# A rebuilt prologue and conv stage in a one-core decoder-trunk step

## The reference

```python
h = x * rsqrt(mean(x * x) + EPS) * norm_mix            # per token
a = h @ w_pw1 + b_pw1                                  # 1024 -> 2048
glu = a[..., :1024] * sigmoid(a[..., 1024:])
full = concat([hist, glu], axis=1)                     # 30 rows of history: zeros (prompt), state (samples)
c = silu(layernorm(causal_dwconv(full, w_dw, b_dw)))   # width 31, one filter per channel
x = x + (c @ w_pw2 + b_pw2)
```

## Time and profile before

| | |
|---|---|
| median of 3 runs | 2673.03 us (2672.75 to 2674.61) |
| span of the profiled execution, first to last instruction | 2671.8 us |
| mean granted TensorE clock | 0.957 |
| TensorE matmul busy (PE) / weight load (PEld) | 2464.1 us (92%) / 2360.2 us (88%) |
| VectorE, ScalarE, GpSimd busy | 1352.7 / 528.5 / 772.3 us |
| PE on the chain that ended last | 82% of the span |

### The profile page before, as it was taken

One profiled execution on the slowest core, in us unless ns is written; L12 is line 12 of the kernel. 1 busy time (PEld: TensorE's weight loads), 2 busy tenths in 40 slices (PEclk: granted clock), 3 DMA queues, 4 the chain that ended last, 5 costly groups with the idle time before them and its releaser, 6 DMA issues.

```text
span 2671.8 us, 37036 instructions
## 1 busy us (share of the span) xinstructions
PE 2464.1 (92%) x14763; PEld 2360.2 (88%) x14763; DVE 1352.7 (51%) x1227; ACT 528.5 (20%) x914; POOL 772.3 (29%) x400
## 2 busy tenths in 40 slices
PE   3899995699999999999989989889999999999996
PEld 2888884699999999999979967679999999999996
DVE  2688887534444444344464656644444433444444
ACT  2432221421011110111030057612111011011113
POOL 0132321332333333333322223322333333333320
PEclk9898987799999999999999979988999999999998
DMA  5010100111111111111111020011111111111111
GB/s 162 24 32 16 31 16 8 40 40 40 48 47 47 40 47 47 47 47 47 40 39 40 16 60 1 9 32 40 40 48 47 47 41 45 47 47 47 41 38 70
DMA packets 156781, 110.93 MB, mean 42 GB/s; under 512 B 6487, under 2 KB 142055, under 8 KB 156599
## 3 DMA queue, kind: packets, MB, share of 16 engines
q1 hardware_dynamic: 154352, 98.90, 14.4%
q10 hardware_dynamic: 2371, 11.21, 1.4%
HBM read 105.20 MB, written 8.10 MB: 42 GB/s over the span
## 4 chain that ended last, share of the span: by engine, by line
PE 82%; DVE 9%; ACT 3%; issue 3%; DMA 1%; ACTq 1%; DVEq 0%; POOL 0%
PE PS L1398 53%; PE PS L1416 15%; PE PS L1501 5%; DVE CONV L778 2%; PE PS L1289 2%; PE PS L1450 2%; PE PS L1320 2%; PE PS L1292 1%; DVE X L693 1%; ACT WK L1147 1%; DVE WK L874 1%; DMA WK<-in_state_ffn 1%; PE PS L1557 1%; PE PS L1523 1%; DVE WK L666 1%
## 5 line engine op out<-in xcount | busy, mean ns | idle before, releaser
L1398 PE MATMUL PS<-H,W 128*128 128x344 f32 x9504 | 1531.3, 323 | 47.6 <-DVE H L854 21.9
L1398 PEld LDWEIGHTS PS<-H,W 128*128 128x128 f32 x9504 | 1518.0, 190 | 54.4 <-issue 34.2
L450 POOL CAST W<-RAW 128x1024 fp32r<-128x1024 f32 x176 | 195.2, 1109 | 1580.1 <-issue 782.1
L1416 PE MATMUL PS<-MID,W 128*128 128x344 f32 x3168 | 513.7, 322 | 20.4 <-DVE X L693 10.5
L1416 PEld LDWEIGHTS PS<-MID,W 128*128 128x128 f32 x3168 | 504.5, 190 | 27.0 <-DVE X L693 16.5
L452 POOL TENSOR_TENSOR W<-RAW,W 128x1024 fp32r<-128x1024 f32 x176 | 477.8, 2715 | 14.1
L693 DVE TENSOR_TENSOR X<-PS,X 128x1032 f32<-128x1032 f32 (+1 forms) x184 | 226.2, 1230 | 231.2 <-PE PS L1416 183.4
L778 DVE SCALAR_TENSOR_TENSOR CONV<-WK,PAR,CONV 128x1024 f32 (+1 forms) x152 | 223.9, 1473 | 18.0 <-DVE CONV L778 2.0
L898 DVE TENSOR_TENSOR WK<-PS,WK 128x1032 f32<-128x1032 f32 x44 | 54.3, 1233 | 299.9 <-PE PS L1398 297.6
L1154 ACT ACTIVATE MID<-WK 128x1032 fp32r<-128x1032 f32 x44 | 47.1, 1070 | 678.2 <-DVE WK L900 678.2
L874 DVE TENSOR_TENSOR WK<-PS,WK 128x1032 f32<-128x1032 f32 x44 | 54.3, 1233 | 224.0 <-PE PS L1398 223.9
(11 more groups left out here) (173 smaller groups left out, 1547.8 us busy)
## 6 DMA issues: line engine op xcount, KB each, us to landing
RAW<-in_ffn_w_in SPq DMA_DIRECT2D x176, 256.0 KB, 3.9
RAW<-in_ffn_w_down SPq DMA_DIRECT2D x88, 256.0 KB, 3.8
RAW<-in_conv_w_pw SPq DMA_DIRECT2D x48, 256.0 KB, 4.0
RAW<-in_attn_w_qkv SPq DMA_DIRECT2D x24, 256.0 KB, 3.8
XIN<-in_x_prompt ACTq DMA_DIRECT2D x8, 512.0 KB, 13.2
RAW<-in_attn_w_o SPq DMA_DIRECT2D x32, 128.0 KB, 2.8
out_y_prompt<-YOUT SPq DMA_DIRECT2D x8, 512.0 KB
WK<-in_const_rope ACTq DMA_DIRECT2D x1, 1032.0 KB, 5.3
```

The costliest lines, as they stand in the source:

```text
L450: nc.gpsimd.tensor_copy(W[:, slot, 0, :], RAW[:, slot, :]).then_inc(s_hi, hi.up())
L1398: last = matmul(PS[:, 3 * side + c, 0:CH], W[:, slot, wp, k * P:(k + 1) * P], H[:, hp, k, c * CH:(c + 1) * CH], start=(k == 0 and q == 0), ...
L1416: last = matmul(PS[:, 3 * side + c, 0:CH], W[:, slot, wp, t * BANK + m * P:t * BANK + (m + 1) * P], MID[:, t, hp, c * CH:(c + 1) * CH], st ...
```

## The change

- **Loads.** SP issues x blocks 0 to 3, the first pw1 weight tile, x blocks 4 to 7, the second weight tile, then history rows, a repeated copy of the depthwise weights (`WREP`) and the FFN rows. Each x block has its own semaphore. ScalarE issues 12 row DMAs instead of 20; the four state copies move behind the making of `H`.
- **x, block by block.** TensorE transposes a token block as it lands. ACT squares the same block with a running sum along the row, so token sums need no matmul; `RS` is ready before the first dense group.
- **Normalised H.** DVE makes `X * norm_mix * RS` (`normed_tile`), ACT its high part, DVE its rest. Dense results need no scaling: ACT's sigmoid and DVE's gated product read PSUM directly.
- **First two dense groups together** (`dense_pair`): for each tile of `H`, as it comes, the matmuls of both sides.
- **Late parameters.** FFN rows are transposed after that pair; the sample history becomes a product on POOL and 16 small matmuls (`SHIST`).
- **Taps one tile behind.** TensorE runs both dense groups of tile i, then `last_taps(i - 1)`. DVE does the gated product, 8 taps (NEARLY), `finish_tile(i - 1)`, the rest of `GSPLIT`, 11 taps. The loops are written out straight. Single buffers stay single.

```diff
+            for b in range(NB // 2):
+                x_block(b)
             load(halves(w_pw1, 0), 0)
+            for b in range(NB // 2, NB):
+                x_block(b)
             load(halves(w_pw1, D), 1)
...
+            pool.wait_ge(s_hrows, 16 * HROW_DMAS)
+            for hf in range(2):
+                nc.gpsimd.tensor_tensor(HROWS[hf], HROWS[hf], WREP[0:HALF_B * HIST, :], ALU.mult).then_inc(s_hw, 1)
...
+            for b in range(NB):
+                o = b % 2
+                dve.wait_ge(s_tr, tr.next())
+                v.tensor_copy(X[:, :, b * P:(b + 1) * P].rearrange("p (a m) n -> p a m n", a=2),
+                              PS[:, 2 * o:2 * o + 2, :].rearrange("p a (m n) -> p a m n", m=KT // 2)).then_inc(s_trr, trr.up())
...
+            token_scale()
+            dve.wait_ge(s_bc, bc.next())
+            v.tensor_copy(RS[:, 0:SEQ].rearrange("p (c n) -> p c n", c=2), PS[:, 6:8, :])
+            v.tensor_copy(RS[:, SEQ:T], PS[:, 5, 128:128 + NS]).then_inc(s_bcr, bcr.up())
...
+            def normed_tile(m):
+                v.scalar_tensor_tensor(NORMED[m % 2], X[:, m, :], par(m, R_MIX), RS, ALU.mult, ALU.mult).then_inc(s_n32, n32.up())
+            def normed_lo(m):
+                dve.wait_ge(s_hh, hh.next())
+                v.tensor_tensor(H[:, 1, m, :], NORMED[m % 2], H[:, 0, m, :].bitcast(F32), ALU.subtract).then_inc(s_h, h.up())
+            normed_tile(0)
+            normed_tile(1)
+            for m in range(KT):
+                normed_lo(m)
+                if m + 2 < KT:
+                    dve.wait_ge(s_h, h.at())
+                    normed_tile(m + 2)
...
+            def gated_tile(i):
+                mm.n += 2
+                dve.wait_ge(s_sig, sig.next())
+                if i > 0:
+                    dve.wait_ge(s_gh, gh.at())
                 dve.wait_ge(s_v, own.at())
+                v.scalar_tensor_tensor(chunks(GL[:, HIST:WKC]), side(0), par(i, R_B1), chunks(SIG), ALU.add,
+                                       ALU.mult).then_inc(s_pr, pr.up(2))
...
+            for i in range(KT):
+                gated_tile(i)
+                if i == 0:
+                    late_params()
+                v.scalar_tensor_tensor(CONV[:, i, SEQ:T], GL[:, HIST + SEQ:WKC], par(i, R_DW + HIST), SHIST[:, i, :],
+                                       ALU.mult, ALU.add).then_inc(s_v, own.up())
+                dve.wait_ge(s_tap0, tap0.next())
+                conv_taps(i, 1, 1 + NEARLY)
+                if i > 0:
+                    finish_tile(i - 1)
                 dve.wait_ge(s_gh, gh.next())
                 v.tensor_tensor(GSPLIT[:, 1, 0:WKC], GL[:, 0:WKC], GSPLIT[:, 0, 0:WKC].bitcast(F32), ALU.subtract).then_inc(s_gs, gs.up())
+                conv_taps(i, 1 + NEARLY, CW - NT)
             finish_tile(KT - 1)
...
+            act.wait_ge(s_rows, 16 * ROW_DMAS)
+            F_(JUNK[1][0:NS, :], XS_ROWS, ACT.Square, accum_out=TOK[0:NS, 0, NB:NB + 1]).then_inc(s_a, 1)
+            for b in range(NB):
+                act.wait_ge(s_xb[b], 16)
+                if b > 0:
+                    act.wait_ge(s_a, b)
+                F_(JUNK[b % 2], XIN[:, b, :], ACT.Square, accum_out=TOK[:, 0, b:b + 1]).then_inc(s_a, 1)
...
+            for i in range(KT):
+                act.wait_ge(s_mm, 2 * i + 2)
...
+                F_(chunks(SIG), PS[:, 3:6, 0:CH], ACT.Sigmoid, bias=par(i, R_B1 + 1)).then_inc(s_sig, sig.up())
                 act.wait_ge(s_pr, pr.next(2))
+                F_(CONV[:, i, 0:SEQ], GL[:, 0:SEQ], ACT.Identity, scale=par(i, R_DW), bias=par(i, R_BDW)).then_inc(s_tap0, tap0.up())
+                F_(CKEEP[:, i, :], GL[:, SEQ:WKC], ACT.Copy)
+                if i == 0:
+                    act.wait_ge(s_late, 1)
+                else:
+                    act.wait_ge(s_td, td.next())
                 F_(GSPLIT[:, 0, 0:WKC], GL[:, 0:WKC], ACT.Copy).then_inc(s_gh, gh.up())
+                diagonals(i, DIAGA, 0)
                 diagonals(i, DIAGB, NTA)
...
+            for b in range(NB):
+                o = b % 2
+                pe.wait_ge(s_xb[b], 16)
+                if b >= 2:
+                    pe.wait_ge(s_trr, trr.next())
+                for m in range(KT):
+                    last = transpose(PS[:, 2 * o + m // 4, (m % 4) * P:(m % 4 + 1) * P], XIN[:, b, m * P:(m + 1) * P])
                 last.then_inc(s_tr, tr.up())
...
+            def dense_pair():
+                for n in range(2):
+                    pe.wait_ge(s_w, w.next())
+                    begin_group()
+                for k in range(KT):
+                    pe.wait_ge(s_h, h.next())
+                    for side in range(2):
...
+            def late_params():
+                pe.wait_ge(s_frows, 16 * FROW_DMAS)
+                for f in range(FT):
+                    transpose(PS[:, 7 - f // 12, (f % 12) * 2 * NFR:(f % 12 + 1) * 2 * NFR], FROWS[0:2 * NFR, f * P:(f + 1) * P])
+                pe.wait_ge(s_hw, 2)
+                for m in range(KT):
+                    for hf in range(2):
+                        col = 400 + m * NS + hf * HALF_B
+                        last = matmul(PS[:, 6, col:col + HALF_B], HROWS[hf][:, m * P:(m + 1) * P], KSEL, start=True, stop=True)
+                last.then_inc(s_late, 1)
...
+            dense_pair()
+            late_params()
+            for i in range(1, KT):
+                pe.wait_ge(s_pr, 2 * i)
+                dense(0, 0, wait_taken=False)
+                dense(1, 1, wait_taken=False)
+                last_taps(i - 1)
+            last_taps(KT - 1)
```

More of the change, by code:

```diff
@@ L232, in build @@
         s_rows = sem("rows_loaded")
-        s_x = sem("x_loaded")
+        s_xb = [sem(f"x_block_loaded{b}") for b in range(NB)]
+        s_frows = sem("ffn_rows_loaded")
+        s_hrows = sem("history_rows_loaded")
+        s_hw = sem("history_weighted")
+        s_late = sem("late_params_turned")
+        s_latr = sem("late_params_taken")
+        s_n32 = sem("normed_tile")
         s_tab = sem("tables_loaded")
@@ L441, in _, with split @@
             raw = [Count(), Count()]
-            def split(slot, per, free):
+            def split(slot, per, free, first_pair=False):
                 pool.wait_ge(s_raw[slot], raw[slot].next(per))
-                if free:
+                if free and not first_pair:
                     pool.wait_ge(s_wstart, started.at())
@@ L749, in _ @@
[L749 to L761, removed]
@@ new lines, in normed_lo @@
+            def normed_lo(m):
[8 more added lines that the diff above has]
+                    normed_tile(m + 2)
+            sig, glu, tap0, gh, gs, td, tt = (Count() for _ in range(7))
@@ L1024, in _ @@
[L1024 to L1028 removed]
+                    (XS_ROWS, a["x_sample"].rearrange("b s d -> (b s) d")),
@@ L1084, in diagonals @@
                     F_(D_[:, 0, k, :], IDENT, ACT.Identity, scale=par(i, R_DW + CW - NT + first + k))
-                    lo = TAPLO[:, bass.ds(i, 1), first + k:first + k + 1].rearrange("p a b -> p (a b)")
-                    last = F_(D_[:, 1, k, :], IDENT, ACT.Identity, scale=lo)
+                    last = F_(D_[:, 1, k, :], IDENT, ACT.Identity, scale=TAPLO[:, i, first + k:first + k + 1])
                 last.then_inc(s_diag, diag.up())
-            GL, TG, SIG = (WK[:, k, :] for k in (4, 3, 5))
@@ L1235, in _ @@
                     roots()
-            turned, taken = 1 + KT, 2 + KT
+            turned, taken = TURNED, TAKEN
             ka = Count()
@@ L1464, in _ @@
-            for m in range(KT):
-                last = transpose(PS[:, 7, m * NS:(m + 1) * NS], WK[0:NS, 3, m * P:(m + 1) * P])
-            last = matmul(PS[:, 7, 64:64 + NH], ONES[0:1, :], WK[0:1, 3, D:D + NH], start=True, stop=True)
-            last.then_inc(s_tr, tr.up())
-            pe.wait_ge(s_trr, trr.next(2))
-            pe.wait_ge(s_x, 16 * NB)
-            for m in range(KT):
-                o = m % 2
-                pe.wait_ge(s_trr, trr.at(1))
-                trr.n += 1
-                for b in range(NB):
-                    last = transpose(PS[:, 2 * o + b // 4, (b % 4) * P:(b % 4 + 1) * P], XIN[:, b, m * P:(m + 1) * P])
-                last.then_inc(s_tr, tr.up())
@@ L1503, in last_taps @@
                 last.then_inc(s_td, td.up())
-            dense(0, 0)
-            last_taps()
-            dense(1, 1)
-            with turns(pe, 2, KT, {w: 2, started: 2, mm: 2, pr: 2, gs: 1, diag: 2, td: 1, tt: 1}):
-                dense(0, 0)
-                last_taps()
-                dense(1, 1)
-            last_taps()
+            dense_pair()
+            late_params()
+            for i in range(1, KT):
+                pe.wait_ge(s_pr, 2 * i)
[3 more added lines that the diff above has]
+            last_taps(KT - 1)
             pe.wait_ge(s_cs, KT)
```

284 lines of the change are left out of this document (129 added, 155 removed).

## The result

The changed kernel takes 2601.43 us (median of four runs, 2599.74 to 2603.38); the kernel before takes 2672.89 on the same chip (2669.36 to 2674.61). The ratio is 0.9734, 95% interval 0.972 to 0.9748: 71.5 us faster, against 74 to 75 predicted. The profiled execution took 2603.38 us, its span is 2601.6, its mean granted clock 0.967.

The account below looks back on a forecast made before the run. Matmuls fill 92% of the span, so gains come only where TensorE waits, does needless work or runs below full clock, in the first 450 us. Prologue 40.2 plus tiles 41.7 less tail 7.9 gives 74 us off: 2598, range 2580 to 2626.

Parts of the forecast that it names:

- the first transpose at 20 us or later: Prologue: a sign that the prediction is wrong; the rows were forecast to be in at 12 us.
- rows in: Prologue: the 12 parameter rows land at 12 us, between a lower bound of 8 and an upper one of 28.1.
- small operations, transposes of x: Prologue: 17 small operations take 3.2 us, 64 transposes of x 15.9, ending at 31.1; PE sets this.
- to the first dense matmul: Prologue: last copy, reciprocal, broadcasts, copies to `RS`, two `normed_tile`, one rest and hand-overs; the dense pair starts at 41.
- dense pair: Tile 0's first two dense groups: 22.7 us plus 2.6 for PE's slow start, ending at 66.3 against 106.46.
- late parameters and pair 1: Between tile 0 and tile 1: 9.0 us of transposes and small matmuls on PE, then pair 1 in 22.7.
- six tiles: After pair 1: six times taps and pair at 38.25 us, 229.5 in all; the eighth pair ends at 327.5.
- tail: Eighth pair's end to first layer-norm sum: 49 us, near the 51 with DVE late; 43 with DVE on time.
- rows come late: Prologue rival: rows still land at 28.1 because x competes; everything up to the pair moves by 16, 2614; chance 0.12.
- The estimate from that page: 31-row load on one engine: 4.4 us alone, 8.8 with x in between; rows in near 14, sum 2 us higher.
- a stream swinging between the two levels: Dense pair rival: small pauses keep the clock low; the pair takes 36.5 instead of 25.3, 2609 us; chance 0.07.
- straight code that comes too slowly: Tiles 2 to 7 rival: PE instructions delivered too slowly; above 10.6 us a tile the time passes 2673; chance 0.03.

Follow-up runs that it names:

- both remedies together: Against the changed kernel, the 31-row load is cut into 16 and 15 rows and x waits for the parameter rows: 2592.37 us, ratio 0.9710.

## Why the prediction was right

The total was right by 3.4 us, and the mark at the layer-norm sum by 0.2 (376.5 forecast, 376.68 measured). In part this is chance: terms too large and too small cancelled, and one of the forecast's own signs of being wrong came true (the first transpose at 20 us or later; it stands at 22.42).

| Step | forecast | measured | off by |
|---|---|---|---|
| rows in | 12 | 22.42 | +10.4 |
| small operations, transposes of x | 19.1 | 14.4 | -4.7 |
| to the first dense matmul | 9.9 | 12.1 | +2.2 |
| dense pair | 25.3 | 24.35 | -1.0 |
| late parameters and pair 1 | 31.7 | 32.7 | +1.0 |
| six tiles | 229.5 | 228.8 | -0.7 |
| tail | 49 | 41.9 | -7.1 |

**Rows at 12** was the step that failed most. I put them near the lower bound because the bulky rows had left the queue; what mattered was one 31-row load with x beside it. With x held back the rows are in at 11.2, so two thirds of the rival "rows come late" came true (10.4 of its 16 us). Its sum, 2614, did not come, because other terms fell. By the rule that the prediction cites from the Trainium skill ("DMA: Bandwidth & Descriptors", "Why a DMA increments its semaphore by 16 and not by 1") 16 and 15 rows spread over 16 and 15 engines where 31 sit on one. The trace agrees: the whole load alone kept 0.07 of the 16 engines busy, about one, and the split made it quick. The estimate from that page, 4.4 us alone and the rows in near 14 with x in between, was too short both times: alone they came 8.6 us after the load's issue, with x 8 us later than estimated. That the load in two pieces came in at 14.22 is a coincidence; the estimate was for one piece.

**Transposes of x.** I used 1.99 us for eight, from a kernel in which they ran at that pace. Here all 64 were busy for 10.4, the last ones 1.08 for eight. The granted clock reads 1.00 in both of these stretches, so I cannot say what made them quicker. In the kernel before the next 16 took 0.229 each at a granted 0.51 (54 to 58 us), so the low clock goes with the slow pace there; for the eight that I used it does not show.

**To the pair:** two `normed_tile` took 4.51 instead of 2.58; POOL's history product runs from 40.65 for 4.65 us beside them. I had put that product well before 66 and at no cost. With both remedies together it starts at 33.58, and there the two `normed_tile` that start before it take 2.50 while the two operations of DVE beside it take 3.37 and 3.29, not 1.2 to 1.3: the price moves with the product.

**Pair, late parameters, pair 1.** The pair went as argued, a cold start (granted 0.50 in the first 3.1 us) and then no pauses. The rival drawn from the Trainium skill ("TensorE: Matmul & The Clock Gate", "A second HAM failure mode: psum-queue depth-cycling"), a stream swinging between the two levels, did not come: the clock is 0.97 from 52 to 54 us and 1.00 from 56 to the end of the pair. The late parameters took 7.2, not 9.0, but I left out that their own low clock would reach into pair 1, 2.8 us.

**The tiles** were right in mechanism and size. Taps follow at 1.00 without a wait, and the run with the taps between the groups shows that with the old order on PE and the new one on DVE the whole gain is gone; with the split first on DVE half of it stays. The rival of straight code that comes too slowly did not come: 38.13, against the 38.25 of tile 1 before, which was straight code too.

**Tail.** I took DVE as level with PE (38.8 a tile) and 13.6 late at the end (11 for tile 0 and 3.3 for the rest make 14.3, a slip without weight). It was faster. DVE's taps by shape, 130 to 330 us (5.3 tiles; busy us, mean ns, idle before):

```profile
L836 DVE SCALAR_TENSOR_TENSOR CONV<-WK,PAR,CONV 128x1024 f32<-128x1024 f32 x100 | 169.0, 1690 | 8.4 <-ACT CONV L1124 5.3
```

The taps are slower than I assumed, 1.69 with POOL's stalls in them, 32.1 for 19 (forecast 28.8 and a stall of 2.2). But the idle time is 1.6 a tile, 1.05 of it the wait for tap 0, where I had counted 2.5 and 1.23. The 2.5 were small gaps between the taps of the loop before (14.9 us over 114 taps, 0.13 each), and in straight code they shrink to 0.02 or 0.03 (the chain of the run with the load split lists them). DVE's tile is 37.6 (gated products at 188.50 and 226.13), so it catches up and is 3.3 behind at the eighth pair. The tail then follows the other path that I had worked out, 43 with DVE on time; 41.9 was measured.

**After the conv stage** I expected no difference; 3.5 us net were lost there in this profile, 5.3 at the low clock shown above and the rest by losses and gains behind it.

## What to carry to other kernels

When a consumer waits for a short chain on another engine, list what the chain's engine does first and what the consumer can do meanwhile: here moving one call, or one operation ahead of eight (both counted from the run with the taps between and the split late), was worth 73 and 37 us. PE's visible waits for that chain were less, 53.3 us in that run, 5.4 and 25.4 after the two moves; the rest is in good part matmuls that ran at a lower clock behind a wait. Look at the shapes of small early loads: a 31-row load in two pieces brought the layer-norm sum 5.3 to 5.6 us forward. Time a change at a mark near it as well as in the total, which here moved by up to 5.7 us in code behind the mark that no run had touched. And when a sum comes out right, check its terms: this one had an error of 10 us in one place and of 7 in another.

## What the runs showed that I had not expected

- The 31-row load of 124 KB: the rows were in at 22.42 whole and at 14.22 and 15.35 in two pieces with x beside them, at 11.2 and 6.8 with x held back. Whole, it also delays x (complete at 30.1, split 24.3, both with x transposed first).
- A busy TensorE can lose its clock: 0.69 over 7.2 us of small transposes and matmuls of 4 columns without a gap. The transposes and the first 1.3 us of the matmuls ran at 1.00, the rest at 0.50. No run here has either kind alone.
- Untouched code can come out at another clock: behind 18 matmuls at 1.00 and an idle time of 4.6 us the next group took 19.0 us, behind 18 slow ones and 3.3 us it took 13.7 in the kernel before, but 17.7 behind 18 slow ones and 3.2 us in two experiments. What decides it stays open.
